# Both feed-forwards of a decoder layer by one level of Strassen's algorithm, on one Trainium2 core

## What is computed

```python
x = x + 0.5 * _swiglu(_rmsnorm(x, ffn1_norm_g), ffn1_w_gate, ffn1_w_up, ffn1_w_down)
z = _rmsnorm(x, mix_norm_g) @ w_in               # mLSTM heads and gated-linear-attention heads
x = x + y_mix @ w_out
x = x + cross_attention(_rmsnorm(x, xattn_norm_g), memory keys and values)
x = x + 0.5 * _swiglu(_rmsnorm(x, ffn2_norm_g), ffn2_w_gate, ffn2_w_up, ffn2_w_down)
# _swiglu(x, wg, wu, wd) = (silu(x @ wg) * (x @ wu)) @ wd
```

## Time and profile before

| | |
|---|---|
| median of 3 runs | 1346.64 us |
| span of the profiled execution (first to last instruction) | 1342.9 us |
| PE busy | 1326.3 us, 99% |
| DVE busy | 666.0 us, 50% |
| ACT busy | 430.2 us, 32% |
| POOL busy | 41.9 us, 3% |

### The profile page before, as it was taken

How to read it: one execution, slowest core, us unless ns; L and a number is a source line. 1 busy time by engine, 2 the same in 40 slices (tenths; PEclk the granted TensorE clock), 3 DMA queues, 4 the chain that set the end, 5 groups by cost and what they waited for, 6 DMA issues and landing times.

```text
span 1342.9 us, 25785 instructions
## 1 busy us (share of the span) xinstructions
PE 1326.3 (99%) x11027; PEld 1290.5 (96%) x11027; DVE 666.0 (50%) x906; ACT 430.2 (32%) x647; POOL 41.9 (3%) x64
## 2 busy tenths in 40 slices
PE   8999999999999999999999999999999999999998
PEld 8999999999999999998888899889999999999998
DVE  5444454533333367667766634535545445443333
ACT  6222222222223143335533623323322222222222
POOL 1000000000000000002111000100000000000000
PEclk9999999999999999998999999999999999999999
DMA  6332323223223223224145664523232232323321
...
DMA packets 208137, 138.32 MB, mean 103 GB/s; under 512 B 6550, under 2 KB 196224, under 8 KB 208068
## 3 DMA queue, kind: packets, MB, share of 16 engines
...
...
## 4 chain that ended last, share of the span: by engine, by line
PE 93%; DVE 3%; ACT 2%; issue 1%; DMA 0%; DVEq 0%; ACTq 0%
PE ps L1742 90%; PE ps L2186 1%; DVE lv_qk L1172 0%; ACT w_hi L552 0%; DVE w_lo L990 0%; PE ps L2292 0%; DVE xn_lo L1008 0%; DVE s_st L1400 0%; DVE lv_acc L1186 0%; PE ps L2217 0%; DVE ym_tok L1412 0%; DMA const<-in_consts 0%; PE ps L2013 0%; PE ps L1938 0%; DVE lv_e L1156 0%
## 5 line engine op out<-in xcount | busy, mean ns | idle before, releaser
L1742 PE MATMUL ps<-xn_hi,w_hi 128*128 128x272 f32 x2144 | 447.1, 289 | 0.9 <-ACT xn_hi L574 0.9
L1742 PE MATMUL ps<-xn_hi,w_lo 128*128 128x272 f32 x2144 | 444.2, 288 | 0.0
L1742 PE MATMUL ps<-xn_lo,w_hi 128*128 128x272 f32 x2144 | 442.7, 287 | 0.6 <-DVE xn_lo L1008 0.6
L552 ACT ACTIVATE w_hi<-raw 128x1024 fp32r<-128x1024 f32 x206 | 218.0, 1058 | 642.5 <-PE ps L1742 642.5
L990 DVE TENSOR_TENSOR w_lo<-raw,w_hi 128x1024 fp32r<-128x1024 f32 x206 | 252.4, 1225 | 201.7 <-ACT w_hi L552 200.7
L1742 PEld LDWEIGHTS ps<-xn_hi,w_hi 128*128 128x128 f32 x2144 | 336.2, 188 | 2.1 <-DVE w_lo L990 1.1
L1742 PEld LDWEIGHTS ps<-xn_hi,w_lo 128*128 128x128 f32 x2144 | 337.6, 189 | 0.0
L1742 PEld LDWEIGHTS ps<-xn_lo,w_hi 128*128 128x128 f32 x2144 | 336.2, 188 | 1.0 <-DVE xn_lo L1008 0.8
L1742 PE MATMUL ps<-h_hi,w_hi 128*128 128x272 f32 (+1 forms) x704 | 149.6, 289 | 0.0
L1742 PE MATMUL ps<-h_hi,w_lo 128*128 128x272 f32 (+1 forms) x704 | 148.9, 288 | 0.0
L1742 PE MATMUL ps<-h_lo,w_hi 128*128 128x272 f32 (+1 forms) x704 | 148.6, 287 | 0.0
...
## 6 DMA issues: line engine op xcount, KB each, us to landing
...
```

Of the source, the lines that this page charges most:

```text
L552: act.activation(w_hi[u0 % 2][:, :], raw[u0 % 4][:, :], ACT.Copy).then_inc(sem("hi_done"), 1)
L1742: return pe.matmul(out, lhsT, rhs, start=start, stop=stop)
```

## The change

Each of the matrix products of a feed-forward is cut into 2 x 2 blocks in each operand, over the tokens (272 + 272), over the summed dimension and over the output features, and made by 7 block products of half the size for 8 (the variant with 4 sums on each operand). A *job* is one such product: for gate and up 2 output blocks of 128 over all of the 1024 inputs, for down 2 output blocks over a *chunk* of 6, 8 or 8 of the 22 row blocks. A feed-forward has 11 gate, 11 up and 12 down jobs, 34 jobs or 238 products. A product takes 4 blocks (3 in the down jobs of the first chunk) x 3 matmuls of 272 columns.

What is new on each engine:

- SP loads a job as two DMAs of 512 KB into one of two `raw_job` buffers.
- GpSimd makes the four sums of weight blocks (`sum_weights`, 3 instructions, 4 x 512 elements a partition) and, for 10 of the 11 up jobs of a feed-forward, the four sums of `h` blocks (`h_sums`, 4 instructions of 272). There is one buffer of weight sums, `w_sum0`, for all jobs but the second of each feed-forward.
- ACT and DVE split each of the 7 weight operands of a job, 512 elements each (`prod_hi`, `prod_lo`), into a ring of 4. They run 4 products ahead of PE.
- PE makes product i in one bank of PSUM; the two jobs under way have four banks each. P2 is added onto P1, P4 onto P7, P3 onto P5.
- DVE adds up the 7 products (`evac_u`, `evac_d`, `evac_c`, `evac_a`, `evac_cd`). RMSNorm's factor is now applied to the input: `xf` = x times gain times `rinv`, in 4 blocks, and 4 sums of them. All 7 are split into `xs_hi` and `xs_lo` before the products that use them. The first two jobs run interleaved, product by product.
- The loops of both feed-forwards are written out, not hardware loops. The last output block is no longer made in two token halves.

The core of the diff:

```diff
+        P1, P2, P3, P4, P5, P6, P7 = range(7)
+        ORDER = (P1, P6, P7, P5, P2, P4, P3)
+        FIRST = (P1, P2, P7, P5, P6, P4, P3)
+        BANK = {P1: 0, P2: 0, P6: 1, P5: 2, P3: 2, P7: 3, P4: 3}
+        COMBO = {P1: 2, P2: 0, P3: 1, P4: 6, P5: 3, P6: 4, P7: 5}
+        W_RAW = {P1: 0, P2: 1, P4: 3}
+        W_SUM = {P7: 0, P5: 1, P6: 2, P3: 3}
...
+        CHUNKS = ((0, 3), (6, 4), (14, 4))
+        JOBS = []
+        for n in range(2):
+            for c, (k0, nq) in enumerate(CHUNKS):
+                for t in range(nq):
+                    if t or not c:
+                        JOBS.append(("gate", n, c, t))
+                    JOBS.append(("up", n, c, t))
+                if c + 1 < len(CHUNKS):
+                    JOBS.append(("gate", n, c + 1, 0))
+                    pass
...
+        for n in range(2):
+            for p_ in FIRST:
+                SEQ += [(N_JOB * n, p_), (N_JOB * n + 1, p_)]
+            for J in range(N_JOB * n + 2, N_JOB * (n + 1)):
+                SEQ += [(J, p_) for p_ in ORDER]
+        N_PROD = len(SEQ) // 2
...
+            def load_job(J):
+
+                kind, n, c, t = JOBS[J]
+                k0, nq = CHUNKS[c]
+                if J % N_JOB >= 2:
+                    sp.wait_ge(sem("prod_lo"), 1 + max(AT[J - 2, p_] for p_ in (P1, P2, P4)))
+                    sp.wait_ge(sem("sum_made"), 3 * (J - 1))
...
+            def sum_weights(J):
+
+                hs, W = half_size(J), w_sum[sum_set(J)]
+                before = sum_before(J)
+                r4 = raw_job[J % 2][:, 0:4 * hs].rearrange("p (h e) -> p h e", h=4)
+                pool.wait_ge(sem(f"job_in{J % 2}"), 32 * (J // 2 + 1))
+                if before >= 0 and not sum_set(J):
+                    pool.wait_ge(sem("prod_lo"), 1 + max(AT[before, P7], AT[before, P5]))
+                pool.tensor_tensor(W[:, 0:2, 0:hs], r4[:, 2:3, :].broadcast_to([128, 2, hs]), r4[:, 0::3, :],
+                                   ALU.subtract).then_inc(sem("sum_made"), 1)
+                pool.wait_ge(sem("sum_made"), 3 * J + 1)
+                if before >= 0 and not sum_set(J):
+                    pool.wait_ge(sem("prod_lo"), 1 + AT[before, P6])
+                pool.tensor_tensor(W[:, 2, 0:hs], W[:, 1, 0:hs], r4[:, 0, :], ALU.subtract)\
+                    .then_inc(sem("sum_made"), 1)
+                pool.wait_ge(sem("sum_made"), 3 * J + 2)
+                if before >= 0 and not sum_set(J):
+                    pool.wait_ge(sem("prod_lo"), 1 + AT[before, P3])
+                pool.tensor_tensor(W[:, 3, 0:hs], r4[:, 1, :], W[:, 2, 0:hs], ALU.add)\
+                    .then_inc(sem("sum_made"), 1)
+
+            def h_sums(Q):
+
+                pool.wait_ge(sem("h_made"), Q + 1)
+                pool.tensor_tensor(hf8[:, 6, :], hf8[:, 0, :], hf8[:, 2, :], ALU.add).then_inc(sem("t_made"), 1)
+                pool.tensor_tensor(hf8[:, 4, :], hf8[:, 0, :], hf8[:, 3, :], ALU.subtract).then_inc(sem("t_made"), 1)
+                pool.wait_ge(sem("t_made"), 4 * Q + 1)
+                pool.tensor_tensor(hf8[:, 5, :], hf8[:, 3, :], hf8[:, 6, :], ALU.subtract).then_inc(sem("t_made"), 1)
+                pool.wait_ge(sem("t_made"), 4 * Q + 3)
...
+            def prod_hi(i):
+
+                J, p_ = SEQ[i]
+                hs = half_size(J)
+                if p_ in W_RAW:
+                    act.wait_ge(sem(f"job_in{J % 2}"), 32 * (J // 2 + 1))
+                else:
+                    act.wait_ge(sem("sum_made"), 3 * J + {P7: 1, P5: 1, P6: 2, P3: 3}[p_])
+                if i >= 4:
+                    act.wait_ge(sem("prod_mm"), i - 3)
+                act.activation(ring_hi[i % 4][:, 0:hs], weight(J, p_), ACT.Copy).then_inc(sem("prod_hi"), 1)
...
+            def prod_lo(i):
+
+                J, p_ = SEQ[i]
+                hs = half_size(J)
+                dve.wait_ge(sem("prod_hi"), i + 1)
+                dve.tensor_tensor(ring_lo[i % 4][:, 0:hs], weight(J, p_), ring_hi[i % 4][:, 0:hs].bitcast(F32),
+                                  ALU.subtract).then_inc(sem("prod_lo"), 1)
...
+            def xf_first(gain):
+
+                for d in range(4):
+                    ins = dve.scalar_tensor_tensor(out=xf[:, 3, d, :], in0=x[:, d, 0:HT],
+                                                   scalar=gains[:, gain + d:gain + d + 1], in1=rinv[:, 0:HT],
+                                                   op0=ALU.mult, op1=ALU.mult)
+                ins.then_inc(sem("xf_made"), 1)
+
...
+            def evac_u_of(J, k):
+
+                dve.wait_ge(sem("prod_mm"), k + 1)
+                dve.wait_ge(sem("a_copied"), J + 1)
+                u = evac_u[J % 2]
+                dve.tensor_tensor(u[:, :], evac_a[J % 2][:, :], ps[:, bank_of(J, P6), 0:HT], ALU.add)\
+                   .then_inc(sem("u_made"), 1)
...
+            def evac_cd_of(J, k):
+
+                kind, q = JOBS[J][0], bank_of(J, P3)
...
+                    dst = gt if kind == "gate" else hf8
+                    dve.tensor_tensor(dst[:, 0:2, :], CD, u[:, :].unsqueeze(1).broadcast_to([128, 2, HT]), ALU.add)\
+                       .then_inc(sem("cd_read"), 1)
+                if kind == "up":
+                    Q = quad_of(J)
+                    dve.wait_ge(sem("cd_read"), J + 1)
+                    dve.wait_ge(sem("silu_rest"), Q + 1)
+                    dve.tensor_tensor(hf8[:, 0:3, :], hf8[:, 0:3, :], gt[:, 0:3, :], ALU.mult)\
+                       .then_inc(sem("h_made"), 1)
...
+            def product(i):
+
+                J, p_ = SEQ[i]
+                kind, n, c, t = JOBS[J]
+                nk = half_size(J) // 128
+                pe.wait_ge(sem("prod_lo"), i + 1)
+                if J % N_JOB >= 2:
+                    if p_ == P1:
+                        if JOBS[J - 2][0] == "gate":
+                            pe.wait_ge(sem("silu_a"), quad_of(J - 2) + 1)
...
+                        pe.wait_ge(sem("u_made"), J - 1)
+                    if p_ in (P7, P5):
+                        pe.wait_ge(sem("cd_read"), J - 1)
+                if p_ == P2:
+                    pe.wait_ge(sem("a_copied"), J + 1)
+                if p_ == P4:
+                    pe.wait_ge(sem("d_read"), J + 1)
+                if p_ == P3:
+                    pe.wait_ge(sem("c_read"), J + 1)
+                if J % N_JOB < 2:
+                    pe.wait_ge(sem("xs_lo_done"), 7 * n + FIRST.index(p_) + 1)
+                hi, lo = (hs_hi, hs_lo) if kind == "down" else (xs_hi, xs_lo)
+                dst, m = ps[:, bank_of(J, p_), 0:HT], COMBO[p_]
+                wh, wl = ring_hi[i % 4], ring_lo[i % 4]
+                start = p_ in (P1, P5, P6, P7)
+                for j in range(nk):
+                    if kind == "down" and j == nk - 1:
+                        Q = NF // 2 * n + (CHUNKS[c][0] // 2 + CHUNKS[c][1] - 1)
+                        pe.wait_ge(sem("hs_lo_done"), 2 * Q + (1 if m < 3 else 2))
+                    cols_ = slice(128 * j, 128 * j + 128)
+                    mm(dst, wh[:, cols_], hi[:, m, j, :], start and j == 0, False, not start)
+                    mm(dst, wl[:, cols_], hi[:, m, j, :], False, False, not start)
+                    ins = mm(dst, wh[:, cols_], lo[:, m, j, :], False, j == nk - 1, not start)
+                ins.then_inc(sem("prod_mm"), 1)
...
+            norm(0, B_N1)
+            pe.wait_ge(evac, 1)
+            spin(24, 7)
+            for i in range(N_PROD):
+                product(i)
...
+            norm(3, B_N4)
+            pe.wait_ge(evac, B_N4 + 1)
+            spin(24, 7)
+
```

More of the change, by code:

```diff
@@ new lines, in quad_of, with adders_to, sum_set, sum_before @@
+        def quad_of(J):
+            return NF // 2 * JOBS[J][1] + CHUNKS[JOBS[J][2]][0] // 2 + JOBS[J][3]
+        def adders_to(J):
+            return sum(j[0] != "gate" for j in JOBS[:J + 1])
+        def sum_set(J):
+            return 1 if J % N_JOB == 1 else 0
+        def sum_before(J):
+            J -= 1
+            while J >= 0 and sum_set(J):
+                J -= 1
+            return J
+        def weight(J, p_):
+            hs = half_size(J)
+            if p_ in W_RAW:
+                return raw_job[J % 2][:, W_RAW[p_] * hs:(W_RAW[p_] + 1) * hs]
+            return w_sum[sum_set(J)][:, W_SUM[p_], 0:hs]
@@ L391, in _ @@
               .then_inc(raw_ready[(U_IN + 1) % 4], 16)
[L392 removed]
+            for k in range(8):
+                src = w_in[:, :, COL_GQ + 128 * k:COL_GQ + 128 * k + 128]
+                if k < 2:
+                    load_first(Z_GQ + k, src)
+                else:
+                    load((Z_GQ + k) % 4, src, Z_GQ + k - 3)
             load_blocks(w_in, U_IN + TURN[Z_MQ], 2, COL_MQ)
@@ L1074, in add_block @@
+            ffn(0)
+            dve.wait_ge(sem("cd_read"), N_JOB)
+            for m in range(2):
+                norm_lo(1, G_MIX, 6 + m)
+            split(U_IN + 1)
+            for m in range(2):
+                add_square(6 + m)
             def add_block(d, buf, scale):
```

726 lines of the change are left out of this document (418 added, 308 removed).

## The result

The changed kernel takes 1449.16 us (median of 4 runs, 1448.16 to 1450.35) against 1346.76 us: ratio 1.0758, 95% interval 1.0742 to 1.0773. It is 7.6% slower; forecast were 1325 us and a range that ended at 1390. The profiled execution has a span of 1448.3 us.

A forecast was written before the change was run, and what follows sets the result against it. TensorE was taken as the bound, busy 99% of the span. 1342.9 - 98.8 (matmuls) + 30 (starts) + 9.5 (seams) + 1 (hand-over) + 36 (GpSimd) = 1320.6 us of span, median 1325 us, range 1284 to 1390.

The forecast's parts named there:

- TensorE, -98.8 us: Both feed-forwards: 792 fewer matmuls at 0.1247 us each come off the span one for one, -98.8 us.
- VectorE's steady load, 17.5 us of 20.95: Gate and up pairs: VectorE's instructions take 17.5 us of the 20.95 us that TensorE needs, 84%.
- rival C: Up jobs: VectorE's order alone lets TensorE run dry, without GpSimd; 20 us more, 1308 us; chance 0.08.
- Rival A: GpSimd and VectorE don't disturb each other, TensorE stays fed except at the seams; no +36, 1288 us; chance 0.28.
- GpSimd, +36 us: 22 gate and up pairs: GpSimd sums and VectorE instructions with two SBUF operands exclude each other, +1.65 us a pair.
- the forecast's own formula: Gate and up pair: 12.97 us of VectorE's two-SBUF-operand instructions plus GpSimd's sums of 5184 elements, 22.6 us against 20.95.
- rival B: Shared SBUF reading becomes the bound, with waits at `w_sum0`; pairs take 25.0 us, total 1382 us; chance 0.27.
- turning point of 2.05 ns an element: GpSimd sum rate from which rival B decides, where gate and up pairs lose 2.6 us each.
- the down jobs pay nothing: Down jobs: exclusion costs 0, since VectorE and GpSimd together have 5.8 + 3.8 us of 10.5.
- the 4.7 each: Seam behind the last up job: down products wait for `h`, a stall of 4.7 us, twice, +9.5 us.
- hidden "at either bound": Gate and up jobs: GpSimd by itself is hidden; P6's operand ready at 6.7 us, 9.1 with three passes, needed by 10.4.
- The starts, +30: Start of both feed-forwards: first product waits for `rinv`, `xf` and `xs`; 14.2 us and 15.8 us, together +30.

The follow-up runs named there:

- no sums: Changed kernel with all of GpSimd's sums left out, raw blocks standing in for the operands (output not the layer's): 1310.55 us, ratio 0.9729.
- fills: Changed kernel with each GpSimd sum replaced by a GpSimd fill that reads nothing, with the same waits: 1351.69 us, ratio 1.0034.

## Why the prediction was wrong

*TensorE, -98.8 us: right.* With the GpSimd work out of the way 478 matmuls start in 60 us, 0.1255 us each; the page counts 10321 records against 11027, 706 fewer. The sum would be 792 fewer and 96 new idle ones, 696.

*VectorE's steady load, 17.5 us of 20.95: right.* 48.29 of 60 us is 80%, forecast 84%; next to nothing is lost at the end of an up job (3.1 us in 38 periods with no sums), so rival C falls. Rival A, no disturbance and 1288 us, falls by the splits of 1.50 us. Its time is 22 us too low even for the kernel with no sums: what stands above 1244.1 there is 65.5 us of span where A, like the forecast without its +36, had 40.5; the last chunk (7.0) and the interleaved jobs (6.8) were put at nothing.

*GpSimd, +36 us: this is the step that failed.* I had the mechanism, full exclusion, and sized it too small three times over. What the sums cost, the change less no sums in the table, is 138.7 us of span where the forecast had 36. First the rate: I took two passes, 1.86 ns an element. An undisturbed sum, at the start of the first feed-forward, GpSimd's time line:

```profile
13.67 2.36 POOL L552 TENSOR_TENSOR w_sum<-raw_job 128x1024 f32<-128x1024 f32 x1
16.11 1.33 POOL L557 TENSOR_TENSOR w_sum<-w_sum,raw_job 128x512 f32<-128x512 f32 x1
17.52 1.31 POOL L562 TENSOR_TENSOR w_sum<-raw_job,w_sum 128x512 f32<-128x512 f32 x1
```

That is 5.00 us for 2048 elements, 2.44 ns each. "GPSIMD Engine Reference" of the Trainium skill, section "Elementwise — side-by-side cycle accounting", has 4497 ns for 2048 elements, 2.2 ns each; the trace is above it, 2.30 for the sum of 1024 and 2.6 for those of 512. With 2.44 the forecast's own formula gives 12.97 + 5184 x 0.00244 = 25.6 us a pair, and 25.5 were measured. That is rival B, with 25.0, and its turning point of 2.05 ns an element was passed. The 38 periods of the table are 19 pairs; 19 x 4.6 is 87, and 85.3 were measured. So in the gate and up jobs the rate, put right, gives the size of the loss. That it comes within 2 us is partly luck: the `h` sums, at 0.82 us for 272 elements, cost 3.0 ns an element and not 2.44, which would make 26.3 us a pair; the formula has no overlap of successive instructions; and in these 38 periods (482 us) neither a GpSimd sum nor a two-operand VectorE instruction runs in 45 us. So the two engines' summed time is most of the pace, not all of it, and waits in the chain through ScalarE are in it too.

Second, "the down jobs pay nothing" was the same sum with 1.86. They lost 25.4 us in the first two chunks. A down job of 512 has 5.8 us on VectorE and 2048 x 2.44 = 5.0 on GpSimd, 10.8 of 10.5. Five of the eight periods of the second chunk are 11.55 to 11.57 us; the first of each feed-forward is longer (14.81 and 13.63), one is 9.64. Why the five take 0.8 us more than the 10.8 wasn't taken apart. In the last chunk the next norm's work comes on top (19.3 us, forecast 0; 7.0 with no sums).

Third, I had the exclusion only in the pairs. It also lengthens the starts and the seams. At the seam VectorE itself makes the h sums while GpSimd makes weight sums. VectorE at the second one:

```profile
1375.76 0.43 DVE L1363 TENSOR_TENSOR hf<-hf 128x272 f32<-128x272 f32 x1
1376.12 2.58 DVE L1364 TENSOR_TENSOR hf<-hf 128x272 f32<-128x272 f32 x1
1378.62 1.49 DVE L1366 TENSOR_TENSOR hf<-hf 128x272 f32<-128x272 f32 x1
```

One sum takes 0.43 and the next 2.58; on GpSimd L552 started at 1375.99 and took 2.41. The seams came to 18.5 us instead of 9.5; with no sums they are 9.8, so the 4.7 each was right for what it counted.

*The chain through GpSimd, hidden "at either bound": wrong in part.* I had compared P6's operand, ready at 6.7 to 9.1 us, with its need at 10.4, and not the instructions queued behind the wait on ScalarE. 4.9 us of weight fills a job and 4.7 of `h` fills an up job cost 37 us of span (41 of the medians) by themselves, and half of it nothing. This is a term of its own that no rival had priced. Since the `h` fills were 1.4 us too long, it is an upper bound for the prediction's case.

*The starts, +30: 34.2 with no sums, 44.4 measured.* First product of the change, TensorE:

```profile
22.23 8.16 PE L2080 MATMUL ps<-const 128*128 128x128 f32 x48 [1.12 <-ACT sig L726]
31.19 0.36 PE L2080 MATMUL ps<-xs_hi,ring_hi 128*128 128x272 f32 x1 [0.80 <-DVE xs_lo L1264]
```

Forecast was 26.7 for the product at 31.19, and 5.8 us for the 48 idle records, which took 8.16 in a stretch with a granted clock of 0.81 (20 to 40 us). Most of these 4.5 us have nothing to do with sums. With no sums the product still starts at 30.05, and there it stands right behind the idle matmuls, which the forecast had over in time:

```profile
22.79 7.50 PE L2071 MATMUL ps<-const 128*128 128x128 f32 x48 [4.92 <-ACT sig L717]
30.05 0.37 PE L2071 MATMUL ps<-xs_hi,ring_hi 128*128 128x272 f32 x1
```

The 10.2 us between 34.2 and 44.4 are again the exclusion, 4.0 in the first start and 6.2 in the second. In the first, `xf`, with x and `rinv` both in SBUF, took 4.16 us for its first four pieces beside a GpSimd sum of 4.69, and 1.74 with no sums.

```profile
18.80 4.69 POOL L552 TENSOR_TENSOR w_sum<-raw_job 128x1024 f32<-128x1024 f32 x1
```

```profile
22.89 4.16 DVE L1239 SCALAR_TENSOR_TENSOR xf<-x,gains,rinv 128x272 f32<-128x272 f32 x4 [1.63 <-ACT rinv L728]
```

In the second, the first four splits took 7.87 us beside the weight sums of the first two jobs, where four undisturbed ones take some 2.5:

```profile
989.79 7.87 DVE L1231 TENSOR_TENSOR ring_lo<-raw_job,ring_hi 128x512 fp32r<-128x512 f32 x4
```

*Rival B's price, 1382 us:* the right mechanism and place and nearly the right pair (25.0 for 25.5). The 70 us of span that it lacks are the down jobs (44.7 us measured, 5 given), the starts (14), the seams (9), the interleaved jobs (9) and 2 of the rest, less 4 in the pairs. So the range ended too low: its upper end was priced almost in one stage alone, and every stage with such sums pays.

Two things stay open. How the 97 us between fills and sums divide into waiting of VectorE and waiting of GpSimd isn't told apart, since either lengthens the other, and fills of the undisturbed length of the `h` sums weren't run. And whether VectorE's load with all sums can be cut below the 20.95 us of a pair wasn't tried.
